# Round zero of the routed experts taken out of its loop, and products of zeros behind five variances

## The reference

```
h = rmsnorm(x, ln1_g) * (1 + sc1) + sh1
x = x + g1 * (concat(lru(h), attention(h)) @ w_out)
h = rmsnorm(x, ln2_g) * (1 + sc2) + sh2
x = x + g2 * (swiglu(h) in layer 0, moe(h) in layer 1)
```

```
logits = h @ router;  vals, idx = top_k(logits, 2);  w = softmax(vals)
y = sum over e of gates[:, e] * ((silu(h @ wg[e]) * (h @ wu[e])) @ wd[e])     # width 3072
```

## Time and profile before

| | us |
|---|---|
| median of 3 runs | 2738.79 |
| the runs | 2738.79, 2739.47, 2729.83 |
| the profiled execution | 2733.64 |
| its span (first to last instruction) | 2731.8 |
| mean granted TensorE clock in it | 0.975 |
| busy: PE, DVE, ACT | 2607.7, 1989.0, 1386.6 |

### The profile page before, as it was taken

How to read it: one execution, slowest core, us unless ns; L and a number is a source line. 1 busy time by engine, 2 the same in 40 slices (tenths; PEclk the granted TensorE clock), 3 DMA queues, 4 the chain that set the end, 5 groups by cost and what they waited for, 6 DMA issues and landing times. The chain is left out here.

```text
span 2731.8 us, 42309 instructions
## 1 busy us (share of the span) xinstructions
PE 2607.7 (95%) x14622; PEld 2253.1 (82%) x14622; DVE 1989.0 (73%) x2726; ACT 1386.6 (51%) x1692; POOL 0.2 (0%) x4
## 2 busy tenths in 40 slices
PE   8979887999999999999898999999999999999998
PEld 3769777888788889999787999877888888888887
DVE  6769325989678877777663664538898898898987
ACT  3355123223444444444443443427777777777775
POOL 0000000000000000000000000000000000000000
PEclk8989899999999999999999999999999999999999
DMA  6631123542668888787351555409999999999996
GB/s 247 216 116 47 47 101 125 158 137 73 202 239 298 295 289 278 253 285 253 114 180 52 181 181 179 172 20 328 351 363 343 353 361 340 354 350 351 374 340 232
DMA packets 223722, 626.83 MB, mean 229 GB/s; under 512 B 15344, under 2 KB 23568, under 8 KB 223376
## 3 DMA queue, kind: packets, MB, share of 16 engines
q1 hardware_dynamic: 223632, 625.64, 65.4%
HBM read 619.29 MB, written 6.29 MB: 229 GB/s over the span
## 5 line engine op out<-in xcount | busy, mean ns | idle before, releaser
L3209 DVE TENSOR_TENSOR wide_low<-wide,wide_high 128x2048 fp32r<-128x2048 f32 x288 | 657.1, 2289 | 96.8 <-ACT wide_high L3091 94.5
L3091 ACT ACTIVATE wide_high<-wide 128x2048 fp32r<-128x2048 f32 x288 | 552.2, 1918 | 184.1 <-PE bank L2946 116.6
L229 DVE TENSOR_TENSOR expert_tile_low<-slot,expert_tile_high 128x1024 fp32r<-128x1024 f32 x216 | 263.7, 1223 | 128.5 <-ACT expert_tile_high L221 124.1
L221 ACT ACTIVATE expert_tile_high<-slot 128x1024 fp32r<-128x1024 f32 x216 | 227.4, 1054 | 189.1 <-PE bank L238 81.6
L2942 PE MATMUL bank<-wide_high,xg_high 128*128 128x512 f32 x768 | 303.6, 395 | 4.3 <-ACT wide_high L3091 4.3
L2943 PE MATMUL bank<-wide_high,xg_low 128*128 128x512 f32 x768 | 300.3, 391 | 0.0
L2946 PE MATMUL bank<-wide_low,xg_high 128*128 128x512 f32 x768 | 206.0, 390 | 0.0
L237 PE MATMUL bank<-h_high,expert_tile_high 128*128 128x256 f32 x704 | 173.2, 284 | 0.0
L238 PE MATMUL bank<-h_low,expert_tile_high 128*128 128x256 f32 x704 | 172.7, 283 | 0.0
L1843 PE MATMUL bank<-expert_tile_high,act_hi 128*128 128x512 f32 x512 | 161.2, 396 | 11.9 <-DVE act_lo L1984 11.9
L2942 PEld LDWEIGHTS bank<-wide_high,xg_high 128*128 128x128 f32 x768 | 144.6, 188 | 33.0 <-ACT wide_high L3091 4.5
(11 more groups left out here) (515 smaller groups left out, 5100.9 us busy)
## 6 DMA issues: line engine op xcount, KB each, us to landing
wide<-in_moe_gu SPq DMA_DIRECT2D x192, 1024.0 KB, 6.1
wide<-in_moe_d SPq DMA_DIRECT2D x96, 1024.0 KB, 6.6
slot<-in_peer_u SPq DMA_DIRECT2D x128, 512.0 KB, 4.3
slot<-in_peer_v SPq DMA_DIRECT2D x128, 512.0 KB, 4.4
slot<-in_w_in SPq DMA_DIRECT2D x72, 512.0 KB, 3.5
picked_or_ada<-in_ada_w SPq DMA_DIRECT2D x48, 512.0 KB, 4.8
ada_slot<-in_ada_w SPq DMA_DIRECT2D x48, 512.0 KB, 4.5
slot<-in_ffn_gu SPq DMA_DIRECT2D x48, 512.0 KB, 3.3
```

Of the source, the lines that this page charges most:

```text
L221: core.nc.scalar.activation(self.tile_hi[:, place % 2], core.slot[u][:], ACT.Copy).then_inc(self.hi_ready.sem, 1)
L229: core.nc.vector.tensor_tensor(self.tile_lo[:, place % 2], slot[:], self.tile_hi[:, place % 2].bitcast(F32), ALU.subtract)\
L3091: nc.scalar.activation(w_hi[n % NB][:].rearrange("p c n -> p (c n)"), wide[n % U][:], ACT.Copy).then_inc(hi_ready.sem, 1)
L3209: nc.vector.tensor_tensor(w_lo[n % NB][:].rearrange("p c n -> p (c n)"), wide[n % U][:], w_hi[n % NB][:].rearrange("p c n -> p (c n)").bit ...
```

## The change

1. A helper `idle_products(core, bank, n)` issues n products of `zeros` with itself into a bank that nobody reads then, with no semaphore. It is called with n = 3 in five places of TensorE's program: behind the variance of `FromExperts`, behind `first.tensor` and behind `second.tensor` of both layers.
2. Round 0 of the routed experts stands ahead of the loop on PE, ACT and DVE, which now runs from 1. In round 0 there is no split of outputs, no scatter and no addition; the fills of the output banks, of `shares_of_places` and of `back` are gone; the semaphores that they moved are raised by hand (`sem_inc`). The wait for the table of rounds moves behind round 0 on PE and ACT. The high part of weight tile 0 is made ahead of `copy_gathered(0)` on ACT, its low part ahead of `take_shares(0)` and `low_gathered(0)` on DVE. TensorE waits for each half of the gathered tokens ahead of the tile that reads it, in all rounds, where it waited for both ahead of the round. SyncE's program is as it was.

```diff
+def idle_products(core, bank, n):
+    for i in range(n):
+        core.nc.tensor.matmul(core.bank[bank][:, :].rearrange("p (o n) -> p o n", o=4), core.zeros[:],
+                              core.zeros[:].rearrange("p (o n) -> p o n", o=1).broadcast_to([P, 4, P]), start=True, stop=True)
...
         last.then_inc(self.var_ready.sem, 1)
+        idle_products(core, 7, 3)
...
             first.tensor(pe)
+            idle_products(core, 7, 3)
...
             second.tensor(pe)
+            idle_products(core, 1, 3)
...
-            pe.wait_ge(table_made.sem, table_made.at(1))
-            with pe.Fori(0, n_rounds(pe)) as k:
-                pe.wait_ge(x_ready.sem, x_ready.at(2) + k * 2)
+
+            def round_(k):
+                first_round = isinstance(k, int)
                 for j in range(J):
                     for w, banks in enumerate((G, UP)):
-                        if j == 1:
+                        if j == 1 and not first_round:
                             pe.wait_ge(added.sem, added.at(2 + 2 * w) + k * C)
                         for half in range(2):
                             at = lambda s: 4 * half + s
+                            if j == 0 and w == 0:
+                                pe.wait_ge(x_ready.sem, x_ready.at(half + 1) + k * 2)
...
-                        if j == 0 and w == 0:
+                        if j == 0 and w == 0 and not first_round:
                             scatter(k)
...
+            pe.sem_inc(scattered.sem, 4)
+            round_(0)
+            pe.wait_ge(table_made.sem, table_made.at(1))
+            with pe.Fori(1, n_rounds(pe)) as k:
+                round_(k)
...
-                    if n == 1:
+                    if n == 1 and not isinstance(k, int):
                         keep_outputs(k)
...
+            act.sem_inc(y_kept.sem, 2)
+            high_tile(0, 0)
+            copy_gathered(0)
+            round_(0)
+            act.wait_ge(table_made.sem, table_made.at(1))
+            with act.Fori(1, n_rounds(act)) as k:
+                round_(k)
...
-            dve.wait_ge(flips.sem, flips.at(4))
-            nc.vector.memset(of_places[:], 0.0)
-            nc.vector.memset(core.bank[Y[1]][:, :], 0.0)
-            nc.vector.memset(core.bank[Y[0]][:, :], 0.0).then_inc(y_made.sem, 1)
-            for tt in range(2):
-                ins = nc.vector.tensor_copy(back[:, tt * P:tt * P + P], core.zeros[:].bitcast(F32))
-            ins.then_inc(backs.sem, 1)
-            take_shares(0)
-            low_gathered(0)
...
+            dve.sem_inc(y_split.sem, 2)
+            dve.sem_inc(y_made.sem, 1)
+            dve.sem_inc(backs.sem, 1)
+            dve.sem_inc(added.sem, 8)
+            low_tile(0, 0)
+            take_shares(0)
+            low_gathered(0)
+            round_(0)
+            with dve.Fori(1, n_rounds(dve)) as k:
+                round_(k)
```

More of the change, by code:

```diff
@@ L2979, in turn @@
                 pe.wait_ge(hid_made.sem, hid_made.at(j + 1) + k * J)
-                if j < 2:
+                if j < 2 and not isinstance(k, int):
                     pe.wait_ge(added.sem, added.at(8) + k * C)
-                else:
+                elif j >= 2:
                     pe.wait_ge(hid_ready.sem, hid_ready.at(j - 1) + k * J)
@@ L2991, in turn_pick @@
                 pe.wait_ge(columns.sem, columns.at(1) + k)
-                pe.wait_ge(y_split.sem, y_split.at(2) + k * 2)
+                if not isinstance(k, int):
+                    pe.wait_ge(y_split.sem, y_split.at(2) + k * 2)
                 for tt in range(2):
@@ L3080, in _, with high_tile, round_ @@
                 nc.scalar.activation(ht[:, q // 2, 512 * (q % 2):512 * (q % 2) + 512], core.bank[4 + q][:, :], ACT.Copy).then_inc(flips.sem, 1)
-            copy_gathered(0)
-            act.wait_ge(table_made.sem, table_made.at(1))
-            with act.Fori(0, n_rounds(act)) as k:
+            def high_tile(k, n):
+                act.wait_ge(wide_landed[n % U].sem, wide_landed[n % U].at(16 * (n // U + 1)) + k * (16 * T // U))
+                act.wait_ge(used.sem, used.at(n + 1) + k * T)
+                nc.scalar.activation(w_hi[n % NB][:].rearrange("p c n -> p (c n)"), wide[n % U][:], ACT.Copy).then_inc(hi_ready.sem, 1)
+            def round_(k):
                 for n in range(T):
@@ L3088, in _ @@
                         nc.scalar.activation(sg[:, j % 2, :], core.bank[G[j % 2]][:, :], ACT.Silu).then_inc(silued.sem, 1)
-                    act.wait_ge(wide_landed[n % U].sem, wide_landed[n % U].at(16 * (n // U + 1)) + k * (16 * T // U))
-                    act.wait_ge(used.sem, used.at(n + 1) + k * T)
-                    nc.scalar.activation(w_hi[n % NB][:].rearrange("p c n -> p (c n)"), wide[n % U][:], ACT.Copy).then_inc(hi_ready.sem, 1)
+                    if n > 0 or not isinstance(k, int):
+                        high_tile(k, n)
                     if n in (10, 14, 18, 22, 26, 28):
@@ L3111, in make_pick @@
             def make_pick(k):
-                e = 0 if isinstance(k, int) else expert_of(dve, k)
+                e = k if isinstance(k, int) else expert_of(dve, k)
                 for tt in range(2):
@@ L3195, in _, with low_tile, round_ @@
             tables(steps)
-            dve.wait_ge(flips.sem, flips.at(4))
-            nc.vector.memset(of_places[:], 0.0)
-            nc.vector.memset(core.bank[Y[1]][:, :], 0.0)
-            nc.vector.memset(core.bank[Y[0]][:, :], 0.0).then_inc(y_made.sem, 1)
-            for tt in range(2):
-                ins = nc.vector.tensor_copy(back[:, tt * P:tt * P + P], core.zeros[:].bitcast(F32))
-            ins.then_inc(backs.sem, 1)
-            take_shares(0)
-            low_gathered(0)
-            with dve.Fori(0, n_rounds(dve)) as k:
-                for n in range(T):
[L3207 to L3211, removed]
+            def low_tile(k, n):
+                dve.wait_ge(used.sem, used.at(n + 1) + k * T)
+                dve.wait_ge(hi_ready.sem, hi_ready.at(n + 1) + k * T)
+                nc.vector.tensor_tensor(w_lo[n % NB][:].rearrange("p c n -> p (c n)"), wide[n % U][:],
+                                        w_hi[n % NB][:].rearrange("p c n -> p (c n)").bitcast(F32), ALU.subtract).then_inc(lo_ready.sem, 1)
+            def round_(k):
+                for n in range(T):
+                    if n > 0 or not isinstance(k, int):
+                        low_tile(k, n)
+                    if n == 1 and not isinstance(k, int):
                         for b in range(2):
                             low_outputs(k, b)
-                    if 3 <= n < 7:
+                    if 3 <= n < 7 and not isinstance(k, int):
                         for m in range(2 * n - 6, 2 * n - 4):
```

## The result

Seven executions of the kernel after have a median of 2716.52 us (2712.78 to 2724.67), seven of the kernel before 2733.38 (2729.11 to 2739.47). The measured ratio is 0.9948 with a 95% interval of 0.9935 to 0.9961: 14 us less, give or take 3.6; the two medians lie 16.9 us apart, which is inside that. The forecast was 2720.5, with 2712 to 2731 as its range.

A forecast was written before the change was run, and what follows sets the result against it. TensorE, busy 95% of the span, was taken as the bound. Terms 2.8 + 2.9 + 1.7 + 3.6 + 1.7 + 1.9 − 0.5 = 14.1 us off 2733.64 gave 2719.5, raised to 2720.5 for run differences; range 2712 to 2731.

The forecast's parts named there:

- Passage: Passage from the experts: zeros cut 3.41 idle us to about 1 and keep the clock up; gain 2.8 us.
- layer 0's first norm: First six tiles behind this norm, 23.6 us, run at full clock in 20.7; gain 2.9 us.
- router: Behind layer 1's second norm: the router's 16 products take 3.62 us at full clock, not 5.30; gain 1.7 us.
- Layer 0's second norm: Feed-forward's entry: 4 of 6.5 idle us remain, clock drop expected, 0 taken; 2.2 us gained if it stayed high.
- Layer 1's first norm: Clock had not dropped here: gain 0 against this execution, up to 2.9 us against one in which it had.
- Start of round zero: Routed experts: first product at 1854.9, not 1858.53, set by VectorE, whose tables end at 1851.64; gain 3.6 us.
- First tile: Round zero's first weight tile: gap ahead shrinks to 0.6 us, so 2.72 us at full clock, not 4.45; gain 1.7.
- scatter: Round zero's second tile takes 2.72 us without the scatter of zeros, against 4.63 with it; gain 1.9 us.
- Entry of the loop: TensorE's table wait, read of the number of rounds and loop entry between rounds 0 and 1: 0.5 us lost.
- The clock dropping all the same: Rival: low clock behind the norms despite zeros, so they give 0; 2727 us, or 2730 if zeros run low; chance 0.15.
- Starvation: Rival: round zero starts early but waits for weight tiles, giving 1.7 us or less; 2725 to 2726 us; chance 0.13.
- Code fetches: Rival: straight round-zero code and the loop body in round 1 cost four more fetch stalls of 6.1 us; 2744; chance 0.05.

The follow-up runs named there:

- version with early credits: Kernel after with first-half tokens ahead of weight tile 0 on VectorE, semaphore credits raised ahead of the tables, six zeros behind layer 0's second norm: median 2716.46 us, ratio 0.9955.
- tokens-first: Kernel after with VectorE splitting the first half of the tokens ahead of weight tile 0: gather to round 1 110.80 and 109.83 us, against 111.56.

## Why the prediction was right, and where it was not

- **What bounds the kernel.** Right: rounds 1 to 7 did not move, and what TensorE did earlier or not at all came off the end whole.
- **Passage, layer 0's first norm, router.** 2.8, 2.9 and 1.7 us forecast, 2.72, 2.84 and 1.68 measured against the same profile. The zeros took 2.7 us where 2.4 was worked out from half the low-clock row, and the gaps left were 0.8 to 1.2 us as forecast.
- **Layer 0's second norm.** The drop was expected and came, 0 us taken; measured 1.1, since the low stretch was shorter. Of six profiles with three zeros there, four gave 1.1 and two nothing. The 2.2 us that the prediction gave for a clock that stays up came with six zeros.
- **Layer 1's first norm.** 0 was right. The argument beside it was wrong: "comes in most cases" put 2.9 us of the distance to the median of 2738.79 here. Three profiles without zeros were all spared. What makes the runs differ is mostly ahead of the change (11.3 us over thirteen profiles, as above), and seven executions gave a median of 2733.38, beside the profile's 2733.64. So the 1.1 us that I left above the sum had no ground; the sum alone, 2719.5, was nearer.
- **Start of round zero.** 3.6 forecast, 3.36 measured, with the engine named rightly; what failed is the step to 1851.7 for the low part: VectorE idled 0.5 us between the table and it. The tokens' low part then came sooner behind the tile's than worked out, and the two errors offset each other in part. In the version with early credits the first product came 0.14 us sooner than with the tokens-first order alone, and VectorE's idle time between the table and `xg_low` fell from 0.43 to 0.03 us, while the table itself came 0.26 us later. There the gather ends at 3.81 us and the first product starts at 3.84, so nothing is left to gain at this start. I had also put the start down to the new order of tile 0; with the fast gather that is worth 0.6 us.
- **First tile and scatter.** 1.7 and 1.9 forecast, 1.60 and 1.95 measured. The reason given for the first tile was a gap that shrinks to 0.6 us, and that was wrong: I had worked with the slow gather, and with the fast one 2.52 us stay idle. The sign that TensorE would start round zero within 1 us of the gather's end therefore failed. The clock stayed up over this gap in the kernel after, and fell over the same gap in the kernel with one zero, where the tile took 4.33 us. So the 1.6 us are right in part by luck. The tokens-first kernels leave 0.03 to 0.18 us there and kept the clock in all four profiles.
- **Entry of the loop.** 0.5 forecast, 0 measured: 2.72 us from the last tile to round 1. The Trainium skill's queue of 64 instructions ("TensorE: Matmul & The Clock Gate", engine queue depths) would have given that; the trace agrees with its consequence and does not show the depth.
- **Sum.** 14.1 forecast and 15.1 in this pair of profiles (11.6 against the second profile of before); 14 give or take 3.6 by the ratio. The profiles' 15.1 hold two terms other than worked out, 1.1 at the feed-forward's entry that was taken as 0 and 0.5 at the loop's entry that was not lost, against about 0.5 less from the other terms.
- **The rivals.** The clock dropping all the same: in the kernel after at one place of five, for half as long; across the versions also at the gather once and at round zero's first tile once, where no zeros stand. Starvation: not in the kernel after; seen once, 1.1 us, in a version that starts 2.4 us earlier. Code fetches: the instruction queue q8 moved 9 packets over rounds zero and 1, against 5 over the loop's first pass before, and none stalled TensorE: the steps from tile 2 of round zero on agree with those of the same tiles before within 0.03 us.
- **The chances.** The bound of 0.5% lies inside the interval (0.39% to 0.65%), so faster by over 0.5% was met narrowly by the ratio of 0.52% and is not certain.

One reference in the account of the kernel before is off: `mix_layer` begins at L2343.

## What to carry to other kernels

Where TensorE waits for a norm's root, products of zeros in the gap can pay as much as removing work (5.4 to 8.9 us here, by the profile of before they are held against, and 6.6 for round zero against the one with its clock), but its size must be read from the gap: three filled it, six cost 1.2 to 1.6 us in each place of the wrong length and gave 1.1 in the one long gap, one left it to chance. When a loop's first pass is taken out, ask which engine's chain sets the new start; here it was VectorE, and the order of its first steps was worth 2 us. Then ask which gap that leaves, since a gap that nothing fills can still lose the clock. To judge effects of a few us, cut the profiles at milestones on the bounding engine: the whole time of the kernel before varied by 10 us, while stretches in which the clock did the same agreed within 0.1 us. A stretch with another clock does not: A differed by 2.7 us between two profiles of the kernel before.

## What was not expected of the hardware

The activation tables. Before, the loop reloaded them twice in each round; after, there is one load in the whole of the rounds. Groups by line of the routed experts, first before, then after:

```profile
L3091 ACT ACT_TABLE_LOAD x8 | 10.3, 1283 | 1.6 <-DMA wide<-in_moe_gu 1.1 <-issue 0.4
L3088 ACT ACT_TABLE_LOAD x8 | 10.3, 1283 | 0.1
```

```profile
L3110 ACT ACT_TABLE_LOAD x1 | 1.3, 1283 | 0.0
```

The loads at the loop's head and before its first silu are gone: 15 of 1.28 us, 19 us of ScalarE. My reading, which no run tests, is that the same function is now in force at the loop's entry and at its turn. I had expected seven rounds' worth to stay. It gave no time here, since ScalarE waits for TensorE in each round; one of them, on the way to the first product, is part of the 3.4 us.

A gap of 3.75 us left the clock up three times in one place, and one of 2.89 us in the same place with one product of zeros lost it. At round zero's first tile a gap of 2.52 us kept it twice and lost it once. The length of a gap alone does not tell.
